# The middle of the first layer's output product by seven block products, with the modulation tiles spread between

## The reference

```
mod = silu(c) @ ada_w + ada_b                    # shift, scale, gate of the layer, 2048 each
h   = rmsnorm(x, norm_g) * (1 + scale) + shift
...                                              # layer 0: attention and convolution -> mix
x_new = x + gate * (mix @ ev_w_out[e])           # (256 x 2048) @ (2048 x 2048)
```

## Time and profile before

| | |
|---|---|
| median of 3 runs | 3030.12 us (3029.75 to 3031.64) |
| the profiled execution's own time | 3029.57 us |
| its span in the trace | 3027.8 us |
| TensorE busy | 2708.6 us, 89% |
| VectorE busy | 2165.1 us, 72% |
| ScalarE, GpSimd busy | 606.5 us, 916.1 us |
| TensorE's granted clock, mean | 0.945 of 2.4 GHz |
| read from memory | 937.14 MB, 311 GB/s over the span |
| chain that ended last | TensorE 49%, DMA 21%, VectorE 14% |

### The profile page before, as it was taken

One profiled execution on the slowest core, in us unless ns is written; L12 is line 12 of the kernel. 1 busy time (PEld: TensorE's weight loads), 2 busy tenths in 40 slices (PEclk: granted clock), 3 DMA queues, 4 the chain that ended last, 5 costly groups with the idle time before them and its releaser, 6 DMA issues.

```text
span 3027.8 us, 30497 instructions
## 1 busy us (share of the span) xinstructions
PE 2708.6 (89%) x11636; PEld 2146.5 (71%) x11636; DVE 2165.1 (72%) x2942; ACT 606.5 (20%) x1263; POOL 916.1 (30%) x732
## 2 busy tenths in 40 slices
PE   5899899999999999999999999776676667999997
PEld 4778678856587688577888688666666655666665
DVE  8979565777896737622663538999999979556666
ACT  1012141010110111012100021122267777000000
POOL 0100001100000101000110004677776667556664
PEclk9999899999999999989999999888887779999999
DMA  8993367968787733322996439999999997999998
GB/s 357 370 366 143 121 222 308 423 258 356 291 319 296 301 123 115 135 86 99 381 422 264 167 144 422 417 421 421 419 412 421 414 388 251 404 411 413 414 414 350
DMA packets 148160, 943.12 MB, mean 311 GB/s; under 512 B 16448, under 2 KB 16448, under 8 KB 50752
## 3 DMA queue, kind: packets, MB, share of 16 engines
q0 software_dynamic: 102528, 612.41, 50.3%
q1 hardware_dynamic: 44352, 320.66, 27.2%
q10 hardware_dynamic: 1152, 8.32, 0.7%
HBM read 937.14 MB, written 4.19 MB: 311 GB/s over the span
## 4 chain that ended last, share of the span: by engine, by line
PE 49%; DMA 21%; DVE 14%; ACT 6%; POOL 5%; issue 4%; DVEq 0%; SPq 0%; ACTq 0%
PE G L529 29%; DMA acc<-v_rows,proj 7%; PE M L776 5%; DMA aring<-ada 4%; DMA aring<-peer_u,proj 3%; DMA mix<-v_rows,proj 3%; DVE proj L1834 3%; PE B L776 2%; ACT vec L1426 2%; DMA vec<-peer_u,proj 2%; PE M L1023 2%; DVE vec L2314 2%; POOL aring L501 2%; DVE aring L1557 2%; DMA proj<-v_rows,proj 2%
## 5 line engine op out<-in xcount | busy, mean ns | idle before, releaser
L529 PE MATMUL G<-h,ring 128*128 128x256 f32 x3840 | 848.4, 383 | 11.3 <-ACT h L1160 11.3
L529 PEld LDWEIGHTS G<-h,ring 128*128 128x128 f32 x3840 | 734.4, 192 | 116.9 <-issue 15.6
L486 POOL DMA_DIRECT2D aring<-ada x200 | 105.8, 529 | 1327.2 <-DVE mods L1557 1305.6
L1557 DVE CUSTOM_DVE_ANT_0 aring<-aring,acc,vec 128x2048 f32<-128x2048 f32 x168 | 391.3, 2350 | 87.5 <-DMA aring<-ada 85.1
L529 PE MATMUL G<-proj,ring 128*128 128x256 f32 x1568 | 345.5, 382 | 0.9 <-DVE proj L2155 0.9
L529 PEld LDWEIGHTS G<-proj,ring 128*128 128x128 f32 x1568 | 300.1, 192 | 44.7 <-issue 3.3
L501 POOL DMA_INDIRECT aring<-peer_u,proj x130 | 233.4, 1795 | 313.8 <-DVE proj L2248 186.2
L1070 PE MATMUL M<-sq,mix 128*128 128x512 f32 x688 | 301.4, 594 | 0.0
L1070 PEld LDWEIGHTS M<-sq,mix 128*128 128x128 f32 x688 | 203.6, 297 | 89.3 <-ACT mix L1440 0.7
L2286 DVE CUSTOM_DVE_ANT_0 aring<-sq,aring 128x2048 f32<-128x2048 f32 x104 | 236.4, 2290 | 33.4 <-DMA aring<-peer_u,proj 22.9
L2314 DVE SCALAR_TENSOR_TENSOR vec<-acc,dots,vec 128x1024 f32<-128x1024 f32 x149 | 191.3, 1284 | 96.0 <-DMA acc<-v_rows,proj 90.4
(11 more groups left out here) (417 smaller groups left out, 3453.9 us busy)
## 6 DMA issues: line engine op xcount, KB each, us to landing
ring<-weights SPq DMA_DIRECT2D x217, 1024.0 KB, 5.0
aring<-ada POOLq DMA_DIRECT2D x200, 1024.0 KB, 9.5
sq<-v_blocks SPq DMA_DIRECT2D x43, 1024.0 KB, 8.0
proj<-v_blocks SPq DMA_DIRECT2D x21, 1024.0 KB, 8.0
ring<-first SPq DMA_DIRECT2D x16, 1024.0 KB, 7.0
acc<-v_rows,proj POOLq DMA_INDIRECT x151, 9.6
aring<-peer_u,proj POOLq DMA_INDIRECT x130, 13.2
acc<-conds ACTq DMA_DIRECT2D x2, 1024.0 KB, 7.3
```

The lines of the kernel that those rows point to most:

```text
L486: pool.dma_start(aring[:, n % SLOTS, :], ada[a]).then_inc(ada_in[n % SLOTS], 16)
L529: mm = nc.tensor.matmul(bank[:, 0:TOK], lhsT=ring[:, slot, weights_at + t * P:weights_at + (t + 1) * P], rhs=rhs[:, t, :], start=(t == ord ...
L1557: V_.tensor_tensor_reduce(out=tile, in0=tile, in1=vector, scale=1.0, scalar=bias, op0=ALU.mult, op1=ALU.add, accum_out=column).then_inc(ad ...
```

## The change

`MIDDLE` gains an entry for `ev_out`, whose middle eight units are now made by `middle_by_sevens`; the counts that the semaphores are compared with are shifted accordingly. The chunks of those eight units are laid out as for the other middles (same size and number). The residual's squares go to `late_squares` (in `proj`) in place of `sq`, since `sq` holds the sums of weights. The 29 modulation tiles between the mixed values and the next layer are placed anew: 7, then one after each of the weight sums 2 to 7, then 6 and 10 with the residual pieces between. `weight_sums` has a branch for two names that no stream of this kernel has. The rest is moving helpers about.

```diff
-MIDDLE = ("od", "od_out", "w_out")
+MIDDLE = {"ev_out": ("ev_out", 4), "od": ("od", 4), "od_out": ("od_out", 4), "w_out": ("w_out", 4)}
...
-            dense("ev_out", [proj], first=4, count=12)
+            middle_by_sevens("ev_out")
+            dense("ev_out", [proj], first=14, count=2)
...
-            residual_sum(sq)
+            residual_sum(late_squares)
...
-            leave_gated(UNIT0["ev_out"], mod("gate0"))
+            leave_gated_middle("ev_out", mod("gate0"))
...
-            ada_part(1, 3, 6)
-            add_residual("ev_out", 0)
-            ada_part(1, 9, 7)
-            ada_part(2, 0, 1)
-            add_residual("ev_out", 1)
-            ada_part(2, 1, 8)
-            add_residual("ev_out", 2)
-            ada_part(2, 9, 7)
-            add_residual("ev_out", 3)
-            add_residual("ev_out", 4)
...
+            sum_halves(*middle_in["ev_out"])
+            ada_part(1, 3, 7)
+            sum_weights("ev_out", 0)
+            sum_weights("ev_out", 1)
+            for i in range(2, 8):
+                sum_weights("ev_out", i)
+                ada_part(1, 8 + i, 1)
+                if i == 2:
+                    add_residual("ev_out", 0, kept=late_squares)
+            join_middle("ev_out")
+            ada_part(2, 0, 6)
+            add_residual("ev_out", 1, kept=late_squares)
+            add_residual("ev_out", 2, kept=late_squares)
+            ada_part(2, 6, 10)
+            add_residual("ev_out", 3, kept=late_squares)
+            add_residual("ev_out", 4, kept=late_squares)
```

More of the change, by code:

```diff
@@ L92, with middle_unit, middle_chunk @@
 ADA0 = 32 + DT - KEPT
-MIDDLE = ("od", "od_out", "w_out")
-MADE_BEFORE = {"od": 0, "wv": 8, "od_out": 24, "w_out": 32}
-DONE_BEFORE = {"od": 0, "wv": 6, "od_out": 18, "w_out": 24}
+MIDDLE = {"ev_out": ("ev_out", 4), "od": ("od", 4), "od_out": ("od_out", 4), "w_out": ("w_out", 4)}
+MADE_BEFORE = {"ev_out": 0, "od": 8, "wv": 16, "od_out": 32, "w_out": 40}
+DONE_BEFORE = {"ev_out": 0, "od": 6, "wv": 12, "od_out": 24, "w_out": 30}
+HALVES_MADE = {"ev_out": 4, "od": 9, "od_out": 14, "w_out": 19}
+JOINED = {"ev_out": 5, "od": 10, "od_out": 15, "w_out": 20}
+TURNED = {name: i + 1 for i, name in enumerate(MIDDLE)}
+def middle_unit(name):
+    stream, first = MIDDLE[name]
+    return UNIT0[stream] + first
+def middle_chunk(name):
+    stream, first = MIDDLE[name]
+    return CHUNK0[stream] + first
 MOD = {"shift0": 0, "scale0": 1, "shift0c": 2, "scale0c": 3}
@@ L290, in build, with weight_sums @@
         half_sums = sums_at(32)
-        middle_in = {"od": (h, half_sums), "od_out": (proj[:, 16:32, :], sums_at(0)), "w_out": (proj[:, 0:16, :], sums_at(16))}
-        middle_out = [sq[:, 0:1024], sq[:, 1024:2048]]
+        middle_in = {"od": (h, half_sums), "ev_out": (proj[:, 0:16, :], sums_at(16)), "od_out": (proj[:, 16:32, :], sums_at(0)), "w_out": (proj[:, 0:16, :], sums_at(16))}
         late_squares = flat(proj[:, 32:48, :])
-        weight_sums = lambda i: [sq[:, (i % 2) * D + 512 * k:(i % 2) * D + 512 * (k + 1)] for k in range(4)]
+        def weight_sums(name, i):
+            if name in ("gates", "gates_late"):
+                return gate_weight_sums[i % 2]
+            return [sq[:, (i % 2) * D + 512 * k:(i % 2) * D + 512 * (k + 1)] for k in range(4)]
         spare_bank = G[1 - UNIT0["oz"] % 2]
         seven_banks = [M[:, 512 * i:512 * (i + 1)] for i in range(4)] + [B6[:, :], B7[:, :], spare_bank[:, :]]
-        middle_banks = {name: seven_banks[0:6] + [G[1 - UNIT0[name] % 2][:, :]] for name in MIDDLE}
+        middle_banks = {name: seven_banks[0:6] + [G[1 - middle_unit(name) % 2][:, :]] for name in MIDDLE}
         v_tok = [flat(proj[:, 8 * tk:8 * tk + 8, :]) for tk in range(2)]
@@ L679, in attention, with by_sevens, middle_by_sevens @@
                         between[hh]()
+            def by_sevens(name, rhs, sums, banks, c, i, k, n_waits):
+                s1, s2, s3, s4 = sums
+                w11, _, w21, w22 = [ring[:, c % SLOTS, 512 * j:512 * (j + 1)] for j in range(4)]
+                t1, t2, t3, t4 = weight_sums(name, i)
+                products = ((rhs[:, k, 0:P], w11), (rhs[:, 8 + k, 0:P], w21), (s2[:, k, :], t2), (s3[:, k, :], t3),
+                            (s1[:, k, :], t1), (s4[:, k, :], w22), (rhs[:, 8 + k, P:2 * P], t4))
+                pe.wait_ge(w_in[c % SLOTS], 16 * (c // SLOTS + 1))
+                for n, (tokens, columns) in enumerate(products):
+                    for signal, value in n_waits.get(n, ()):
+                        pe.wait_ge(signal, value)
+                    if n == 2:
+                        pe.wait_ge(weights_made, MADE_BEFORE[name] + i + 1)
+                    mm = nc.tensor.matmul(banks[n], lhsT=tokens, rhs=columns, start=(k == 0), stop=(k == 7))
+                    if k == 7 and n < 6:
+                        mm.then_inc(wv_done, 1)
+                mm.then_inc(unit_done, 1)
+            def middle_by_sevens(name):
+                rhs, sums = middle_in[name]
+                stream, first = MIDDLE[name]
+                u = middle_unit(name)
+                for k in range(8):
+                    waits = {}
+                    if k == 0:
+                        waits = {2: ((halves_made, HALVES_MADE[name]),), 6: ((unit_evac, u),)}
+                        if name == "gates_late":
+                            waits[0] = ((unit_evac, u - 2),)
+                    by_sevens(name, rhs, sums, middle_banks[name], middle_chunk(name) + k, k, k, waits)
+                dense(stream, [rhs], first=first + 8, count=1, bank_free=True)
+                pe.wait_ge(halves_made, JOINED[name])
+                out = weight_sums(name, 0)
+                for f in range(8):
+                    for tk in range(2):
+                        mm = nc.tensor.transpose(M[:, f * TOK + tk * P:f * TOK + (tk + 1) * P],
+                                                 out[2 * tk + f // 4][:, f % 4 * P:(f % 4 + 1) * P], ident)
+                mm.then_inc(mid_turned, 1)
+                dense(stream, [rhs], first=first + 9, count=1, bank_free=True)
             pe.wait_ge(consts_in, 16)
@@ L809, in values_by_sevens @@
                         waits = {6: ((unit_evac, UNIT0["wv"]),)}
-                    by_sevens(h, half_sums, seven_banks, CHUNK0["wv"] + i, MADE_BEFORE["wv"] + i, k, wv_done, waits)
+                    by_sevens("wv", h, half_sums, seven_banks, CHUNK0["wv"] + i, i, k, waits)
             values_by_sevens(0)
@@ L1128, in leave_middle @@
             def leave_middle(name, dst, func, gate=None):
[L1130 to L1133, removed]
+                act.wait_ge(mid_turned, TURNED[name])
+                first = MIDDLE[name][1]
+                for f in range(first, first + 8):
+                    nc.scalar.activation(dst[:, f, :], M[:, (f - first) * TOK:(f - first + 1) * TOK], func,
+                                         scale=1.0 if gate is None else gate[:, f:f + 1]).then_inc(unit_evac, 1)
             def leave_gated_middle(name, gate):
@@ L1947, in join_middle @@
                 p1, p2, p6, p7, p5, p3, p4 = middle_banks[name]
-                c11, c12, c21, c22 = [middle_out[tk][:, 512 * n:512 * (n + 1)] for tk in range(2) for n in range(2)]
+                c11, c12, c21, c22 = weight_sums(name, 0)
                 done = lambda n: dve.wait_ge(wv_done, DONE_BEFORE[name] + n)
@@ L1962, in join_middle @@
                 step(tt(c12, c12, p3, ALU.add))
-                dve.wait_ge(unit_done, UNIT0[name] + 12)
+                dve.wait_ge(unit_done, middle_unit(name) + 8)
                 step(tt(c21, c21, p4, ALU.add), on=halves_made)
+            sum_halves(*middle_in["ev_out"])
[14 more added lines that the diff above has]
+            add_residual("ev_out", 4, kept=late_squares)
+            mods_from(1)
+            mods_from(2)
+            normed_into_h(V("norm_g1"), mod("scale1"))
             dve.wait_ge(h_ready, 2 * DT)
@@ L2435, in laid_out @@
     def laid_out(w):
-        if any(w is m for m in (u_, od_out_, w_out_)):
+        if any(w is m for m in (ev_out_, u_, od_out_, w_out_)):
             return middle_chunks(w)
```

15 lines of the change are left out of this document (6 added, 9 removed).

## The result

The changed kernel takes 3044.07 us (median of 7 runs, 3038.31 to 3047.39) beside 3030.12 us of the kernel before (7 runs, 3024.95 to 3034.97). The ratio is 1.0041, with a 95% interval from 1.0027 to 1.0054: slower by 12.4 us by this ratio (the two medians lie 14.0 us apart), where 11 us were forecast. The profiled execution has a span of 3036.5 us (own time 3038.31 us).

The account below looks back on a forecast made before the run. The prediction took ev_out to be bound by transfers in its second half, TensorE close behind; a transfer-bound tail of +11 us on the profiled 3029.57 us gave 3040.6 us (3041 us on the median), range 3035 to 3046 us.

Parts of the forecast that it names:

- What bounds the stage before: In ev_out, 490 to 612 us: transfers bound the second half; TensorE's units end 3 us before the last tile is used.
- TensorE gains 5.5 us off the path: Units 4 to 11 of ev_out: 55.3 us become 49.8 us, but TensorE already ended before the tiles.
- VectorE's walk: VectorE's new order in ev_out, walked through from 491.67 us: TensorE's middle ends at 566.0 us, the join at 567.2 us.
- What is left behind the join: After the seven products are joined in ev_out, 13 of 29 modulation tiles are used and 16 remain.
- The tail: From the join to the last tile: VectorE's 43.8 us gives +7.1 us; transfers, ending at 615.1 us, give +11.1 us.
- The waits for tiles: VectorE's idle time on modulation tiles in ev_out would lie mostly behind the join.
- The pause of TensorE costs nothing more: Before od, the clock is already at 1.2 GHz, so the longer pause adds nothing, within 1.5 us either way.
- The sum: Whole kernel: profiled 3029.57 us plus 11 us is 3040.6 us, or 3041 us on the median.
- that the waits take up the sums: Rival in ev_out: VectorE's 33.4 us of waits absorb all new work; 3029 us, no change; chance 0.08.
- the stalling steps: Rival in ev_out's eight steps: late weight sums cost TensorE up to 3.7 us; 3045 us; chance 0.07.
- slow transfers: Rival behind the join: 16 transfers at 359 GB/s take 46.7 us, shift 18 us, 3048 us; chance 0.04.

Follow-up runs that it names:

- two tiles per step: Changed kernel with two modulation tiles in each of weight-sum steps 2 to 7 and 10 behind the join: 3041.68 us (one run), stage 128.4 us.
- four early: Changed kernel with four modulation tiles moved between the two mixing operations, ten behind the join: 3032.06 us, ratio 1.0003 to the kernel before.
- rebalanced: Changed kernel, six tiles moved ahead of the second mixing operation, ten behind the join, first residual piece at the fifth weight sum: 3025.84 us, ratio 0.9986 to before.

## Why the prediction was right

- *What bounds the stage before*: transfers, with TensorE close behind. Shown by halving the bytes (5.1 us gained, and then TensorE's last unit decides).
- *TensorE gains 5.5 us off the path*: measured 5.4 us, and the pause behind it grew to 21.4 us before the last sums.
- *VectorE's walk*: steps 48.07 us forecast, 48.06 us measured; join 76.3 us after the mixing forecast (567.2 less 490.95 us), 76.4 us measured.
- *What is left behind the join*: 16 tiles, as forecast.
- *The tail*: 43.8 us of VectorE's work, and 47.9 us with transfers; measured 48.8 us. I took the chain of transfers as the bound for the whole tail, and that was right in size but not in kind, so that the closeness is in part luck: VectorE's work is 43.8 us of it, and the transfers add 5.0 us at single tiles, of which 2.9 us go when their bytes are halved. They were full only from 590 us on, not from 572 us as I had written, and the share from 518 to 567 us was 0.92 to 0.94, not under 0.9.
- *The waits for tiles*: I expected them mostly behind the join; it is 4.0 of 7.1 us, and the rest is ahead of the first weight sums.
- *The pause of TensorE costs nothing more*: wrong, by 0.7 us, inside the 1.5 us that I had left for it. The eight sum matmuls were still on the way down with the clock before (3.10 us, granted clock 0.61 in their stretch) and run wholly at 1.2 GHz after (3.78 us).
- *The sum*: 7.1 us (VectorE's work up to the last tile) + 5.0 us (transfers in the tail) + 0.7 us (clock) + 0.2 us (the join) = 13.0 us, against 12.9 us measured for the stage and 12.4 us for the time.
- *The rivals*: that the waits take up the sums fell (only some 22 of 33.4 us could be used); the stalling steps didn't occur, and where they were provoked (two tiles per step) they cost less than they gave (11.0 us at the join, 17.2 us in the tail); slow transfers didn't occur: from 590 to 614 us 417 GB/s were moved. The Trainium skill, "DMA: Bandwidth & Descriptors", section "Where 436 GB/s comes from", would have had 358 GB/s there, a figure that the section gets by dividing the memory's rate between two cores; the trace of this program on one core disagrees after the change as before it.
- *Where the experiments' forecasts missed*: the changed kernel with early tiles. Nine tiles between the mixing operation and the third weight sum needed transfers that weren't there (7.0 us of waits), and in the steps TensorE then waited for weight sums. With seven there, and the residual piece later, it came out.

Shown is that the loss is set by the place of the tiles relative to the join (10, 16 and 22 tiles behind it: +6.8, +12.9, +28.3 us) and by when the join comes, not by the amount of VectorE's work. The join's own time counts as much: with ten tiles behind it in each, it ended 87.4 us (two per step), 82.7 us (four early) and 76.5 us (rebalanced) after the start of the mixing operation, and the stage took 128.4, 125.0 and 117.1 us. Open is a wait of about 2 us late in the tail, at the twelfth tile behind the join (605.52 us), and with half the bytes, when the stretch isn't full, at the thirteenth (604.94 us).

## What to carry to other kernels

Equal idle time and new work on an engine don't cancel if the new work is tied to another engine's steps: walk through the order and count what is left behind the last tied point. Where work of an engine is also the clock of a transfer ring of few buffers, postponing it postpones the loads too (here GpSimd issued none between 561.64 and 571.92 us); first look for idle time ahead of the stage, here 12 us between two operations. A gain on TensorE is worth nothing in a stage whose last wait is for something else; moving four tiles alone took 5.0 us from the stage, and in the orders tried the seven products and their sums added nothing to that.

## What the runs showed of the hardware

The last sum matmuls of the stage (eight instructions of 128x256 in the trace) took 1.89 us without a pause before them, 3.10 us after a pause of 3.7 us, 3.47 us after one of 4.1 us (rebalanced), and 3.78 us after pauses of 5.5 us (four early), 8.7 us (two per step) and 21.4 us (after): a short pause already costs, and the longer ones cost the factor of two (granted clock 1.00 and 0.50). The length of the pause isn't all, though: with no tile in the steps it was 37.0 us, and they took 3.48 us at a granted clock of 0.57; why is open. Runs of one kernel spread over 24 us (3017 to 3041 us over 25 and 29 runs of the kernel before, on two chips), while the length of a single stage repeated within 0.6 us between two profiled executions (134.6 and 135.2 us; 116.7 us twice), so small changes are better read as a stage length than as a time.
